# One core, a conv/gating/experts block and an attention block: a small projection moved ahead of the experts, some weight loads cut into parts, and the next stage's weight split interleaved

## What is computed

```
x = x + concatenate([y_conv, y_sgu]) @ w_out                   # "out1"
t = rmsnorm(x, g_ffn)
g_idx = top_1(softmax(t @ w_group)); e_idx = top_2(t @ w_router[g_idx])   # the routing
y = sum over experts e of comb[:, e] * ((silu(t @ w_gate[e]) * (t @ w_up[e])) @ w_down[e])
x = x + y
gate = sigmoid(rmsnorm(x, g_ple) @ w_ple_gate)                 # 1024 x 1024, "pgate"
x = x + gate * (p @ w_ple_proj)                                # 256 x 1024, "pproj"
x = rmsnorm(x, g_final);  x = second_block(x)                  # its first weights: "in2"
```

## Time and profile before

| | us |
|---|---|
| median of 3 runs | 1017.83 (1016.74 to 1020.61) |
| the profiled execution | 1015.59 |
| its span in the profile | 1013.9 |
| PE busy | 950.6 |
| DVE busy | 499.4 |
| ACT busy | 329.8 |

### The profile page before, as it was taken

How to read it: one execution, slowest core, us unless ns; L and a number is a source line. 1 busy time by engine, 2 the same in 40 slices (tenths; PEclk the granted TensorE clock), 3 DMA queues, 4 the chain that set the end, 5 groups by cost and what they waited for, 6 DMA issues and landing times.

```text
span 1013.9 us, 14195 instructions
## 1 busy us (share of the span) xinstructions
PE 950.6 (94%) x5926; PEld 675.0 (67%) x5926; DVE 499.4 (49%) x868; ACT 329.8 (33%) x525; POOL 36.0 (4%) x39
## 2 busy tenths in 40 slices
PE   5999799999999999999898799999988899999997
PEld 5997534544444444443433589978988899999885
DVE  6694512122222323232221666979887567767642
ACT  5723210100100000000000646545555545545531
POOL 1000000000000000000000000222210000000000
PEclk9999799999999999999999899999999989999999
DMA  9957789999999999999999933442433424455401
GB/s 356 399 225 275 305 345 431 409 432 431 431 430 430 431 431 429 430 431 430 431 431 426 380 115 135 176 157 84 167 113 135 169 104 166 168 181 208 152 1 41
DMA packets 23622, 289.45 MB, mean 285 GB/s; under 512 B 2561, under 2 KB 4865, under 8 KB 6017
## 3 DMA queue, kind: packets, MB, share of 16 engines
q1 hardware_dynamic: 22832, 286.91, 69.1%
q10 hardware_dynamic: 720, 1.57, 0.4%
HBM read 287.43 MB, written 1.05 MB: 285 GB/s over the span
## 4 chain that ended last, share of the span: by engine, by line
PE 80%; DVE 9%; DMA 5%; ACT 3%; issue 2%; SPq 0%; DVEq 0%; ACTq 0%
PE ps L270 79%; DMA arena<-in_moe 4%; DVE wl L266 3%; DVE arena L1457 1%; ACT wh L259 1%; DMA ring<-in_w_in 1%; PE ps L960 1%; DVE arena L548 0%; ACT arena L1756 0%; DVE arena L1085 0%; DVE arena L1663 0%; DVE arena L1799 0%; DVE arena L352 0%; ACT arena L1759 0%; PE ps L474 0%
## 5 line engine op out<-in xcount | busy, mean ns | idle before, releaser
L270 PE MATMUL ps<-ring,arena 128*64 128x512 f32 x1232 | 339.9, 597 | 7.6 <-issue 7.6
L270 PEld LDWEIGHTS ps<-ring,arena 128*64 128x64 f32 x1232 | 108.9, 137 | 167.8 <-issue 165.6
L266 DVE TENSOR_TENSOR wl<-ring,wh 128x1024 fp32r<-128x1024 f32 x150 | 181.2, 1238 | 59.4 <-ACT wh L259 59.3
L270 PE MATMUL ps<-arena 128*64 128x512 f32 (+4 forms) x432 | 163.0, 528 | 1.6 <-DVE arena L1085 0.5
L259 ACT ACTIVATE wh<-ring 128x1024 fp32r<-128x1024 f32 x150 | 151.5, 1050 | 35.0 <-PE ps L270 28.6
L1071 DVE SCALAR_TENSOR_TENSOR arena<-ps,arena 128x512 f32<-128x512 f32 x16 | 12.0, 750 | 214.1 <-PE ps L270 214.1
L270 PE MATMUL ps<-up_h,wh 128*128 128x256 f32 x352 | 88.1, 285 | 4.5 <-DVE up_l L1880 4.5
L270 PEld LDWEIGHTS ps<-arena 128*64 128x64 f32 (+2 forms) x432 | 57.4, 146 | 48.5 <-issue 42.7
L270 PE MATMUL ps<-up_l,wh 128*128 128x256 f32 x352 | 87.7, 284 | 0.0
L270 PEld LDWEIGHTS ps<-up_h,wh 128*128 128x128 f32 x352 | 67.4, 191 | 4.9 <-issue 4.9
L1144 ACT ACTIVATE y_h<-ps 128x512 fp32r<-128x512 f32 x32 | 19.1, 597 | 158.3 <-PE ps L270 158.3
(11 more groups left out here) (260 smaller groups left out, 1516.1 us busy)
## 6 DMA issues: line engine op xcount, KB each, us to landing
ring<-in_moe SPq DMA_DIRECT2D x77, 2048.0 KB, 21.5
arena<-in_moe SPq DMA_DIRECT2D x19, 2048.0 KB, 26.1
ring<-in_w_in SPq DMA_DIRECT2D x12, 2048.0 KB, 8.8
ring<-in_w_up SPq DMA_DIRECT2D x11, 2048.0 KB, 7.9
ring<-in_w_dn SPq DMA_DIRECT2D x5, 2048.0 KB, 7.8
ring<-in_w_out SPq DMA_DIRECT2D x4, 2048.0 KB, 15.3
ring<-in_w_pg SPq DMA_DIRECT2D x2, 2048.0 KB, 22.5
ring<-in_w_in SPq DMA_DIRECT2D x2, 1024.0 KB, 10.1
```

Source lines behind the costliest of these rows:

```text
L266: e.tensor_tensor(wl(i), raw_piece(i), wh(i), SUB).then_inc(*lo.up(i))
L270: return e.matmul(o, l, r, start=first, stop=final, skip_group_check=True)
```

## The change

Five things, all in one diff. (1) `pproj` moves in `stream()` from behind the twelfth expert block to ahead of the first, into slot 2, and its products move to `route_pe`: twelve ahead of the counting products, four behind them. The slots of the expert blocks are shifted by one place. (2) d of pair 1 and g of pair 2 are issued in parts into the slots of pair 0's g and u, while these are still used: after row blocks 1, 3, 5 and 7 of g a quarter of each of the two blocks, after row blocks 3 and 7 of u a half. (3) g, u and d of pair 15 and pgate's first block are issued in quarters of 4 KB per partition, each with a semaphore of its own, and `half` and `down` of pair 15 wait for each quarter where they first use it; `down(15)` runs over its row blocks outside and over the two column halves inside. (4) `four` waits at its start for wh alone and uses wl after all products with wh; DVE makes the first two wl pieces between its last y_l and adds. pgate's block is laid out so that a piece is contiguous. (5) In out1, x1_lo(0) moves behind R2's reciprocal, and the squares of the second half's first part ahead of x1_hi(0).

```diff
-N0 = 7
-N1 = N0 + 97
-SLOTS = ([0, 1, 2, 3, 8, 0, 1], [2, 3, 8, 0, 1, 9, 5, 7, 4, 6], [2, 3, 0, 1])
+N0 = 8
+N1 = N0 + 96
+SLOTS = ([0, 1, 2, 3, 8, 0, 1, 2], [3, 8, 0, 1, 9, 5, 7, 4, 6, 2], [2, 3, 0, 1])
...
         def four(e, outs, name, n, xh, xl, ready, first=None, at=None):
...
                 e.wait_ge(*hi.at(i0 + j))
-                e.wait_ge(*lo.at(i0 + j))
+                if first is None:
+                    e.wait_ge(*lo.at(i0 + j))
             if first is not None:
                 for c in range(8):
                     e.wait_ge(*first.at(c))
                     for j in range(4):
                         mm(e, outs[j], wh(i0 + j)[:, c, :], xh[:, c, :], c == 0, False)
+                for j in range(4):
+                    e.wait_ge(*lo.at(i0 + j))
+                    for c in range(8):
                         mm(e, outs[j], wl(i0 + j)[:, c, :], xh[:, c, :], False, False)
...
         def route_pe(e):
+            e.wait_ge(*loaded("pproj", 0))
+            e.wait_ge(l_pT, 16)
+            for h in range(3):
+                project_p(h)
             e.wait_ge(*masked.at(0))
...
+            project_p(3)
...
             def half(q, key):
...
                 if bk == 0:
+                    if q == 0:
+                        e.wait_ge(*pp.at(3))
...
                 for c in range(8):
+                    if q == NP - 1 and c % 2 == 0:
+                        quarter_here(key, c // 2)
...
+                    if q == 0 and (key, c) in part.n:
+                        k.then_inc(*part.up(key, c))
...
                     rest(q, 1)
+                    split_lo(e, FIRST + 1)
                     add(q, 0)
+            split_lo(e, FIRST + 2)
             add(NP - 1, 1)
...
         def loads(e):
...
+                if (name, n) in (("d", 3), ("g", 5)):
+                    key = "g" if name == "d" else "u"
+                    steps = [x for z, x in part.keys if z == key] + [7]
+                    width = SLOT // len(steps)
+                    for x, c in enumerate(steps):
+                        e.wait_ge(*(part.at(key, c) if c < 7 else gu.at(0, key)))
+                        sl = slice(x * width, x * width + width)
+                        for (a, b), to in ((other, place[i - 1][0]), ((dst, src), k)):
+                            e.dma_start(a[:, sl], b[:, sl]).then_inc(
+                                ring_sem[to] if c == 7 else l_bb if name == "d" else l_ws, 16)
+                    continue
...
+                elif name in ("g", "u", "d") and n == NE - 1:
+                    for x in range(4):
+                        sl = slice(x * 1024, x * 1024 + 1024)
+                        for (a, b), to in ((other, place[i - 1][0]), ((dst, src), k)):
+                            e.dma_start(a[:, sl], b[:, sl]).then_inc(l_quarter[name][x][0] if x < 3 else ring_sem[to], 16)
```

More of the change, by code:

```diff
@@ L176, in build @@
         WL = nc.alloc_sbuf_tensor_at("wl", [128, 8, 1024], R32, offset=ring_at + 24 * SLOT)
-        pieces = [(key, j) for key in order[:N0] + order[N1:] for j in range(2 if key == ("fdn", 5) else 4)]
+        pieces = [(key, j) for key in order if key[0] not in ("g", "u", "d", "pproj") for j in range(2 if key == ("fdn", 5) else 4)]
         n_piece = {k: i for i, k in enumerate(pieces)}
-        FIRST = 4 * N0
+        FIRST = n_piece[("pgate", 0), 0]
         P = ([("in1", 0, j) for j in range(4)] + [("in1", 1, i) for i in range(2)]
@@ L225, in wl, with quarter @@
             return piece_view(WL[:, i % 8, :], pieces[i][0][0])
+        def quarter(name, x):
+            if x == 3:
+                return loaded("pgate", 0)
+            return l_quarter[name][x]
         def last_in(k):
@@ L251, in split_hi @@
                     e.wait_ge(s_half, 16)
+                elif (name, m) == ("pgate", 0):
+                    e.wait_ge(*quarter("pgate", j))
                 elif j == 0:
@@ L609, in out1_dve @@
             recip(e, "r2", R2)
+            x1_lo(e, 0)
         r2sum = sig("r2sum", [0])
@@ L729, in build, with project_p @@
         logit = sig("logit", range(2))
+        pp = sig("pp", range(4))
+        PB = (7, 5, 6, 0)
         def route_pe(e):
+            w = slot("pproj", 0).rearrange("p (c n) -> p c n", c=4)
+            def project_p(h):
+                for y in range(2):
+                    for c in range(2):
+                        k = mm(e, ps[PB[h]][:, y * 256:y * 256 + 256],
+                               w[:, c, (2 * h + y) * 128:(2 * h + y) * 128 + 128], PT[:, c, :], c == 0, c == 1)
+                k.then_inc(*ppm.up(h))
+            e.wait_ge(*loaded("pproj", 0))
+            e.wait_ge(l_pT, 16)
+            for h in range(3):
+                project_p(h)
             e.wait_ge(*masked.at(0))
@@ L933, in places, with quarter_here @@
                     weigh(q + 1)
+            def quarter_here(key, x):
+                if x < 3:
+                    e.wait_ge(*quarter(key, x))
+                else:
+                    for n in (NE - 2, NE - 1):
+                        e.wait_ge(*loaded(key, n))
             def half(q, key):
@@ L970, in down @@
                         e.wait_ge(*acc.at(q - 1, 1 + n))
+                    if q < NP - 1:
+                        for f in range(4):
+                            part(n, f)
+                if q == NP - 1:
                     for f in range(4):
[L972 to L975, removed]
+                        quarter_here("d", f)
+                        for n in range(2):
+                            part(n, f)
             def scatter(q, n):
@@ L993, in scatter @@
                     k.then_inc(*scat.up(q, z))
[L995 to L1007, removed]
-                    k.then_inc(*ppm.up(h))
             gather(0)
@@ L1119, in moe_act @@
             for q in range(NP):
[L1120 to L1125 removed]
+                if q == 1:
                     v = many(e)
@@ L2073, in loads @@
                     e.wait_ge(*proj.at("in1", 4, 3))
-                if i == 0:
+                if name in ("g", "u", "d") and n == NE - 2:
+                    other = dst, src
+                elif name in ("g", "u", "d") and n == NE - 1:
[3 more added lines that the diff above has]
+                            e.dma_start(a[:, sl], b[:, sl]).then_inc(l_quarter[name][x][0] if x < 3 else ring_sem[to], 16)
+                elif (name, n) == ("pgate", 0):
+                    for x in range(4):
+                        sl = slice(x * 1024, x * 1024 + 1024)
+                        e.dma_start(dst[:, sl], src[:, sl]).then_inc(l_quarter[name][x][0] if x < 3 else ring_sem[k], 16)
+                elif i == 0:
                     dst, src = (v.rearrange("p (c n) -> p c n", c=8) for v in (dst, src))
```

86 lines of the change are left out of this document (46 added, 40 removed).

## The result

| | before | after |
|---|---|---|
| median of 4 runs each, us | 1017.29 (1016.00 to 1020.61) | 1002.77 (1001.91 to 1003.48) |
| the profiled execution, us | 1015.59 | 1001.91 |
| its span, us | 1013.9 | 999.9 |

The ratio is 0.9852, with a 95% interval of 0.9827 to 0.9877: faster by 1.5%. The forecast was 1002.7 for the median and 1000.5 for the profiled execution. The second is 1.4 us too low. The median lies only 0.9 us above the profiled execution, not 2.2 as before, so the two errors cancel, and the agreement of the medians to 0.1 us is luck.

The account below looks back on a forecast made before the run. Products on PE and weight loads were taken to run level in the experts' stage. 10.0 (lead) + 0 (quarters) + 5.1 (gate) = 15.1 us off 1015.59 gives 1000.5; with the median 2.24 above, 1002.7; range 998 to 1008, 8 in 10.

Parts of the forecast that it names:

- The routing: Before pair 0: projection products fill PE's wait, the clock stays full, and pair 0's g starts 2.7 us earlier.
- The cover: In the routing: twelve projection products, 5.36 us, fill PE's wait for the mask, complete but for 0.2 us.
- The stream: Expert loads up to pair 13: filling the hole at 119.4 to 132 brings them 8.5 to 10.1 us forward, taken as 10.0.
- the tenth load: u of expert 3, not in before 119.4 because p's weights hold a slot; issued at 115.5, it costs 4.88 us.
- I take the upper end: For the stream's lead of 8.5 to 10.1 us, 10.0 was chosen, since the slowest of 16 engines still has work.
- Pair 15: Last pair: PE's stop of 3.58 us before it is the overflow branch's, so loads in quarters are worth 0.
- rival (3): The stop before pair 15 waits for the landing, so quarters let PE start earlier, worth 4.3 us: 998.4; chance 0.08.
- The gate: p's gate, behind pair 15's d: products start on wh and the first ple_h alone, so its first 64 end 5.1 us earlier.
- Rival (2): The clock falls before p's gate, which then brings 3.5 us instead of 5.1: 1004.3; chance 0.17.
- Pieces: Loads cut into DMAs with 4 KB rows: each costs 0.28 us more, the last six 1.7; d's last quarter stays hidden.
- rivals (4) and (5): (4) pieces move like 1 KB rows, 1010.7, chance 0.06; (5) each added DMA empties engines briefly, 1023 to 1031, 0.03.
- Rival (1): The lead at pair 13 is only partly there, 3 to 5 of the 10.0 us are lost: 1006.7; chance 0.13.

Follow-up runs that it names:

- The kernels without the stop: The changed kernel with the branch ahead of pair 15 left out: 997.00 us with pair 15's loads in quarters, 1002.07 with them whole.

## Why the prediction was right, and where its sizes were off

**The routing.** Right: the projection's twelve products fill PE's wait, the clock stays at its upper level, the last six entries of the counting products take 0.83 us for 1.47. The cover is complete. Pair 0's g came 3.7 us earlier, 3.2 without the earlier start, for 2.7 predicted: the products ahead of the gather took 8.05 us (106.48 to 114.53) where I had 8.4, and the gather's turn 4.4, as I took it. It decides little, since the stream is the later one.

**The stream: 10.0 predicted, 8.5 measured.** This is the mis-sized term. 8.5 is how much earlier pair 13's g starts. Between the last load ahead of the hole and u of pair 2 the trace's completions on the fastest engine are 39.1 us apart before, 30.9 now. The lead of 8.2 is 12.1 + 2.5 (hole and p) - 4.85 (the tenth load) + 0.3 (the old hole at 146 to 152) - 0.75 (the new one, predicted as up to 1.6) - 1.0 for the eight parts and - 0.1 for the four halves, where I had 0.3 for rows. In 123 to 128 the parts move at 307 to 397 GB/s; whether the queue was short of them there or they are slow isn't told apart. And the second small hole, counted as + 0.8, didn't go: it moved from 190 to 174. Up to pair 13 the earlier start gave 0.5 back and a hole of 0.4 at 178 to 183, gone now, another 0.3, while the slowest engine's lag took 0.5 (3.8 us now, 3.3 before). "I take the upper end" was the step that failed: the reason given, that the slowest engine still has work, doesn't help, since the fastest engine's idle time is never made up; the slowest one's lag behind it at pair 14's d was 3.6 us before and 4.2 now.

**Pair 15.** The stop is the branch's, as read, and quarters brought 0.3 at most by the profiles, 1.2 and 2.0 by the medians of two calls. PE left it 10.0 us earlier, the number forecast for all from pair 13 on, but by luck: 8.5 from the stream, + 1.7 because the clock did not fall behind pair 13's wait (its 32 products of g took 7.1 us; before, 8.80, below), - 0.6 for small waits at pair 14's landings, + 0.4 for a shorter stop. Then the clock stood at its lower level for 6.8 us instead of 3.4, which cost 1.6, less 0.2 for a wait for ScalarE that is gone, and d was 8.6 earlier. The forecast had no term for the clock at either place. Pair 13's g before, in the chain of waits:

```profile
489.03 8.80 PE ps L270 x32
```

The kernels without the stop bear out rival (3) in its other half: with the stop away the quarters gain 3.6 at the gate's start and 5.1 in the medians, where it had 4.3.

**The gate: 5.1 predicted, 5.2 in the profile** (4.95 us behind d's end for 8.57, and the 64 products in 7.67 us for 9.22), 4.2 by the medians. Rival (2) was undersized: that the clock falls ahead of the gate had 1 in 4. It did not in this profile, but in 5 of the 12 profiled executions with the new gate it did, the same kernel's second one among them:

```profile
531.44 0.88 PE L279 MATMUL ps<-ring,arena 128*64 128x512 f32 x1 [3.16 <-issue]
...
561.41 5.56 PE L279 MATMUL ps<-ple_h,wh 128*128 128x256 f32 x32 [0.73 <-ACT ple_h L1362]
```

**Pieces.** 0.28 us a load predicted, 0.13 measured; rivals (4) and (5) are out. d's last quarter landed at 550.41 for 549.9, hidden as said.

**The sum.** Profile: 8.6 at pair 15's d, + 3.6 to the gate's start, + 1.6 from the full clock = 13.8, against 15.1. The mechanisms held, the stream was taken 1.5 too large, and the clock's falls, left out at pairs 13 and 15, nearly cancelled there. Rival (1), which let 3 to 5 of the 10.0 go, was too pessimistic.

## What to carry over

Where loads and products run level, ask of each edit which hole in the stream it fills or tears, and measure a hole on the fastest DMA engine: late work costs the hole, not its length. Read a stop by what is already there when it begins: if the load has landed, the wait is something else's, and a change that should shorten it will look worthless until that is gone. A rare path that is jumped over can cost a stop of PE and the clock behind it, and announcing the branch takes that off without touching the work.

## What the runs showed of the hardware

- A taken branch over 3,476 instructions stopped PE for 3.00 to 3.58 us; over one wait, or announced 202 instructions ahead, for nothing visible.
- The clock can fall after PE has started again, so the first product doesn't tell. After the stop of 3.00 us ahead of pair 15 (whole loads) the first product took 0.61 us, and 0.7 us after the restart the granted clock was 0.50; after 3.14 us (changed kernel) it was 0.50 from 0.9 us before the restart. It stayed there for 3.4 us in seven of the ten profiles with the stop, and for 6.8 in three.
- The length of a wait doesn't decide it. At pair 13 the clock fell around waits of 2.66 to 2.71 us in nine profiles and around 3.44 in a tenth, and stayed up around 2.65, 2.66, 2.68 and 2.78 in four. A fall of 3.4 us costs 1.5 to 1.7 us of products (5.56 for 4.03, 8.80 for 7.09), so this alone scatters a profile by as much.
- The slowest of the 16 DMA engines lagged the fastest by 3.4 to 5.2 us at pair 14's d, differently in each execution. PE starts when the slowest is through (519.85 for a landing at 519.76), so this too moves its waits by up to 1.8 us.
- The start of the program scatters: the logits began between 103.85 and 106.26 us.
